# Solving the within-chunk system of an RWKV-7 scan by forward substitution over two 64-row halves, in place of completing the 128-row inverse

## What is computed

```python
def step(S, inp):
    r_t, w_t, k_t, v_t, kk_t, a_t = inp
    sa = jnp.einsum('bhij,bhj->bhi', S, -kk_t)
    S = (S * w_t[:, :, None, :]
         + sa[..., None] * (kk_t * a_t)[:, :, None, :]
         + v_t[..., None] * k_t[:, :, None, :])
    y = jnp.einsum('bhij,bhj->bhi', S, r_t)
    return S, y

S0 = jnp.zeros((b, RWKV_HEADS, RWKV_HEAD_DIM, RWKV_HEAD_DIM), F32)
_, ys = lax.scan(step, S0, (tmajor(rh), tmajor(wh), tmajor(kh), tmajor(vh), tmajor(kk), tmajor(ah)))
```

## Time and profile before

| | |
|---|---|
| median of 3 runs | 1505.27 us (1505.21 to 1505.7) |
| the profiled execution | 1507.26 us, its span 1505.4 us |
| TensorE busy | 98% of the span |
| VectorE, ScalarE busy | 83%, 67% |
| chunk 0's edited part | 429.9 to 445.2 us |
| chunk 1's edited part | 469.5 to 486.7 us |
| first expert product | 542.01 us |

### The profile page before, as it was taken

The page is one execution under the profiler, slowest core; times in us unless marked ns, Lnnn a source line. Parts: engine busy times, 40 slices in busy tenths (PEclk is TensorE's granted clock), DMA queues, the critical chain, the costliest instruction groups (busy, mean ns, idle before and its releaser), DMA issues.

```text
span 1505.4 us, 22041 instructions
## 1 busy us (share of the span) xinstructions
PE 1474.2 (98%) x8088; PEld 1226.9 (82%) x8088; DVE 1242.6 (83%) x1375; ACT 1009.8 (67%) x1157; POOL 22.2 (1%) x19
## 2 busy tenths in 40 slices
PE   8999999999899999999999999999999999999997
PEld 5888888799798588888888888888888888888885
DVE  3756666787885289999999999999999999999997
ACT  2544444663523178888888888888888878888885
POOL 0000000000000020000000000000000000000200
PEclk9999999999999999999999999999999999999998
DMA  9889553036405499999999999999999999999990
GB/s 361 326 271 301 175 168 112 1 117 217 141 2 178 174 322 372 395 392 395 396 392 396 394 368 388 390 365 383 394 366 373 393 386 362 395 380 362 349 369 28
DMA packets 206696, 453.57 MB, mean 301 GB/s; under 512 B 8881, under 2 KB 46257, under 8 KB 206386
## 3 DMA queue, kind: packets, MB, share of 16 engines
q1 hardware_dynamic: 203154, 446.12, 80.6%
q0 software_dynamic: 1280, 4.20, 1.1%
q10 hardware_dynamic: 2208, 2.50, 0.5%
HBM read 437.58 MB, written 23.60 MB: 306 GB/s over the span
## 4 chain that ended last, share of the span: by engine, by line
PE 92%; DVE 5%; ACT 2%; DMA 1%; issue 0%; DVEq 0%; ACTq 0%
PE psum L1591 20%; PE psum L1593 20%; PE psum L1592 20%; PE psum L2401 5%; PE psum L2404 3%; PE psum L902 2%; PE psum L2325 2%; PE psum L2365 2%; PE psum L2366 2%; PE psum L2367 2%; PE psum L600 2%; PE psum L1609 2%; PE psum L2318 1%; PE psum L696 1%; DVE time_mix_parts L1150 1%; PE psum L722 1%
## 5 line engine op out<-in xcount | busy, mean ns | idle before, releaser
L1799 DVE TENSOR_TENSOR w_lo<-ring,w_hi 128x1024 fp32r<-128x1024 f32 x672 | 811.0, 1224 | 63.5 <-ACT w_hi L1693 15.8
L1693 ACT ACTIVATE w_hi<-ring 128x1024 fp32r<-128x1024 f32 x672 | 711.3, 1062 | 172.5 <-PE psum L1593 172.4
L1591 PE MATMUL psum<-w_hi,xg_split 128*128 128x512 f32 x896 | 353.5, 395 | 0.3 <-DVE xg_split L1890 0.3
L1593 PE MATMUL psum<-w_lo,xg_split 128*128 128x512 f32 x896 | 349.4, 390 | 0.0
L1592 PE MATMUL psum<-w_hi,xg_split 128*128 128x512 f32 x896 | 348.8, 389 | 0.0
L1593 PEld LDWEIGHTS psum<-w_lo,xg_split 128*128 128x128 f32 x896 | 168.1, 188 | 35.8
L1591 PEld LDWEIGHTS psum<-w_hi,xg_split 128*128 128x128 f32 x896 | 168.3, 188 | 34.1 <-DVE xg_split L1890 0.6
L1592 PEld LDWEIGHTS psum<-w_hi,xg_split 128*128 128x128 f32 x896 | 168.4, 188 | 33.6
L1591 PE MATMUL psum<-w_hi,ht_split 128*128 128x512 f32 x448 | 176.0, 393 | 0.0
L1593 PE MATMUL psum<-w_lo,ht_split 128*128 128x512 f32 x448 | 174.6, 390 | 0.0
L1592 PE MATMUL psum<-w_hi,ht_split 128*128 128x512 f32 x448 | 174.4, 389 | 0.0
(11 more groups left out here) (370 smaller groups left out, 1488.7 us busy)
## 6 DMA issues: line engine op xcount, KB each, us to landing
ring<-o_moe_wg_dram SPq DMA_DIRECT2D x56, 2048.0 KB, 10.8
ring<-o_moe_wu_dram SPq DMA_DIRECT2D x56, 2048.0 KB, 11.3
ring<-o_moe_wd_dram SPq DMA_DIRECT2D x56, 2048.0 KB, 11.3
ring<-e_ffn_wg_dram SPq DMA_DIRECT2D x11, 1024.0 KB, 5.5
ring<-e_ffn_wu_dram SPq DMA_DIRECT2D x11, 1024.0 KB, 8.7
ring<-e_ffn_wd_dram SPq DMA_DIRECT2D x11, 1024.0 KB, 11.1
expert_rows<-work SPq DMA_DIRECT2D x1, 8192.0 KB, 27.9
ring<-e_w_in_dram SPq DMA_DIRECT2D x2, 2048.0 KB, 18.1
```

The costliest lines, as they stand in the source:

```text
L1591: nc.tensor.matmul(dst, x_hi, hi, start=first, stop=False)
L1593: return nc.tensor.matmul(dst, x_hi, lo, start=False, stop=last_)
L1693: nc.scalar.activation(w_hi[:, (4 * i + n) % 4, :], piece(i, n), ACT.Copy).then_inc(m_hi, 1)
L1799: V.tensor_tensor(w_lo[:, r, :], piece(i, n), w_hi[:, r, :].bitcast(F32), ALU.subtract).then_inc(m_lo, 1)
```

## The change

The top level of the inverse is taken out. What is left of XT are two inverses of 64 rows on its diagonal, and the system is solved by halves: the top half of U is the top inverse times the top half of R; the product of the matrix's lower left block with it is added to the low half of R on TensorE (third product of a head); then the low inverse gives the low half of U. `turned(c, 2)`, `top_Y` and `top_X` go, with their copies. `right_side` and `solved` run for a pair and a half. ScalarE, not VectorE, copies the solutions, 64 rows at a time, into `Us`, which now lies beside `Rs` in the ring. The masks of chunk 0 come one step earlier in VectorE's list. GpSimd's clearing of `Y6` goes, and with it one wait; so does the wait for the end of `recur(1, r)` ahead of chunk 0's solve.

```diff
-            def top_Y(c):
...
-            def top_X(c):
...
-            def solved(c):
-                for pair in range(2):
-                    pe.wait_ge(t_rc, 2 * c + pair + 1)
-                    pe.wait_ge(l_x6, 2 * c + pair + 1)
-                    for gg, l, k, o, at in heads_of(pair):
-                        last = nc.tensor.matmul(psum[:, (6, 0)[c] + pair, at:at + HD], XT[c][:, gg, l, :],
-                                                Rs[:, gg, HD * l:HD * l + HD], start=True, stop=True)
-                    last.then_inc(t_u, 1)
+            top, low = slice(0, HD), slice(HD, P)
+
+            def solved(c, pair, rows):
+                if rows == top:
+                    pe.wait_ge(l_xd, masked_at(c, 1, pair))
+                    pe.wait_ge(t_rc, 4 * c + pair + 1)
+                else:
+                    pe.wait_ge(t_rc, 4 * c + 2 + pair + 1)
+                for gg, l, k, o, at in heads_of(pair):
+                    last = nc.tensor.matmul(psum[rows, 4 + pair, at:at + HD], XT[c][rows, gg, l, rows],
+                                            Rs[rows, gg, HD * l:HD * l + HD], start=True, stop=True)
+                last.then_inc(t_u, 1)
+
+            def right_side(c, pair, rows):
+                pe.wait_ge(a_pm, 4 * c + 2 * pair + 2)
+                if rows == low:
+                    pe.wait_ge(t_uc, 4 * c + pair + 1)
+                upto = slice(0, rows.stop)
+                for gg, l, k, o, at in heads_of(pair):
+                    dst = psum[rows, pair, at:at + HD]
+                    vv = v_row[upto, c * D + k * P + o:c * D + k * P + o + HD]
+                    last = nc.tensor.matmul(dst, A_all[c][upto, gg, l, 2, rows], vv, start=True, stop=(c == 0 and rows == top))
+                    if c == 1:
+                        last = nc.tensor.matmul(dst, AR[:, k, c, 0, rows], ST[:, k, o:o + HD], start=False, stop=(rows == top))
+                    if rows == low:
+                        last = nc.tensor.matmul(dst, A_all[c][top, gg, l, 0, low], Us[top, gg, HD * l:HD * l + HD],
+                                                start=False, stop=True)
+                last.then_inc(t_r, 1)
...
+            right_side(0, 0, top)
             block_rows(1, 3)
-            turned(0, 2)
-            right_side(0, 0)
-            pe.wait_ge(y_zero, 3)
-            top_Y(0)
+            right_side(0, 1, top)
+            solved(0, 0, top)
+            solved(0, 1, top)
             block_rows(1, 4)
-            right_side(0, 1)
-            top_X(0)
-            pe.wait_ge(rec_done, 2)
-            solved(0)
+            for pair in range(2):
+                right_side(0, pair, low)
+            for pair in range(2):
+                solved(0, pair, low)
             outputs(0)
...
-            turned(1, 2)
-            right_side(1, 0)
-            top_Y(1)
-            right_side(1, 1)
-            top_X(1)
-            solved(1)
+            for rows in (top, low):
+                for pair in range(2):
+                    right_side(1, pair, rows)
+                for pair in range(2):
+                    solved(1, pair, rows)
             outputs(1)
...
+            def solved(c, pair, half):
+                rows = slice(HD * half, HD * half + HD)
+                act.wait_ge(t_u, 4 * c + 2 * half + pair + 1)
+                nc.scalar.activation(Us[rows, 2 * pair:2 * pair + 2, :], r3(psum[rows, 4 + pair, :], 2),
+                                     ACT.Copy).then_inc(t_uc, 1)
...
             recur(1, 3)
+            masked(0, 0)
             level_Y(0, 1, 0)
-            masked(0, 0)
+            masked(0, 1)
             level_Y(0, 1, 1)
-            masked(0, 1)
+            masked(0, 2)
             level_X(0, 1, 0)
-            masked(0, 2)
+            masked(0, 3)
             level_X(0, 1, 1)
-            masked(0, 3)
```

More of the change, by code:

```diff
@@ L416, in trunk @@
         s_part, s_col = sem("column_product"), sem("column_added")
-        l_tr, l_xe, l_y, l_yd, l_ya, l_xu, l_xd, l_x6 = (sem(x) for x in (
-            "level_T", "level_T_copied", "level_Y", "level_Y_masked", "top_Y_copied", "level_X", "level_X_added",
-            "top_X_copied"))
+        l_tr, l_xe, l_y, l_yd, l_xu, l_xd = (sem(x) for x in (
+            "level_T", "level_T_copied", "level_Y", "level_Y_masked", "level_X", "level_X_added"))
         y_zero, b_done, gw_done = sem("level_Y_zeroed"), sem("bonus_gated"), sem("gate_weighted")
@@ L473, in trunk @@
         Xv = [wu(3, 1024, 1024 * v).rearrange("p (g l t) -> p g l t", g=4, l=4) for v in range(2)]
-        Y6 = ru(13, 1024).rearrange("p (g n) -> p g n", g=4)
         Rs = ru(13, 1024, 1024).rearrange("p (g n) -> p g n", g=4)
@@ L477, in trunk @@
         pick = flatT[:, 0:(B0 - 1) * P]
-        Us = flatT[:, 0:1024].rearrange("p (g n) -> p g n", g=4)
+        Us = ru(13, 1024).rearrange("p (g n) -> p g n", g=4)
         gsq = flatT[:, 1024:2048].rearrange("p (k t) -> p k t", k=KT)
@@ L514, in lev @@
         def lev(c, v, pair):
-            return 6 * c + 2 * v + pair + 1
+            return 4 * c + 2 * v + pair + 1
         def masked_at(c, v, pair):
@@ L522, in turned_at @@
         def turned_at(c, v, n):
-            return 12 * c + 4 * v + n + 1
+            return 8 * c + 4 * v + n + 1
         TURN_BANK = (0, 1, 4, 5)
@@ L743, in rwkv_pe @@
             products(15)
-            def right_side(c, pair):
-                pe.wait_ge(a_pm, 4 * c + 2 * pair + 2)
-                pe.wait_ge(l_xe, turned_at(c, 2, pair))
-                for gg, l, k, o, at in heads_of(pair):
[L749 to L754, removed]
             pe.wait_ge(a_ma, 16)
@@ L758, in rwkv_pe @@
                 nc.tensor.transpose(psum[:, 2, 0:P], ident, ident)
-            pe.wait_ge(y_zero, 3)
+            pe.wait_ge(y_zero, 2)
             def turned(c, v):
@@ L766, in turned @@
                             pe.wait_ge(t_sc, 2)
-                    elif v == 2 and gg >= 2:
-                        pe.wait_ge(l_xd, masked_at(c, 1, 1))
                     else:
@@ L826, in outputs @@
             def outputs(c):
                 for pair in range(2):
-                    pe.wait_ge(t_uc, 2 * c + pair + 1)
+                    pe.wait_ge(t_uc, 4 * c + 2 + pair + 1)
                     pe.wait_ge(a_pm, 4 * c + 2 * pair + 2)
@@ L886, in rwkv_pe @@
             level_X(1, 1, 1)
-            turned(1, 2)
-            right_side(1, 0)
-            top_Y(1)
-            right_side(1, 1)
-            top_X(1)
-            solved(1)
+            for rows in (top, low):
[3 more added lines that the diff above has]
+                    solved(1, pair, rows)
             outputs(1)
             pe.wait_ge(t_yc, 4)
-            pe.wait_ge(l_x6, 4)
             gn_mean(1, 4)
@@ L1044, in copied, with right_side @@
                     nc.scalar.activation(a_home(s_), psum[:, bank:bank + 2, :], ACT.Copy).then_inc(a_ma, 1)
-            def right_side(c, pair):
-                act.wait_ge(t_r, 2 * c + pair + 1)
-                nc.scalar.activation(Rs[:, 2 * pair:2 * pair + 2, :], r3(psum[:, pair, :], 2),
+            def right_side(c, pair, half):
+                rows = slice(HD * half, HD * half + HD)
+                act.wait_ge(t_r, 4 * c + 2 * half + pair + 1)
+                nc.scalar.activation(Rs[rows, 2 * pair:2 * pair + 2, :], r3(psum[rows, pair, :], 2),
                                      ACT.Copy).then_inc(t_rc, 1)
+            def solved(c, pair, half):
+                rows = slice(HD * half, HD * half + HD)
+                act.wait_ge(t_u, 4 * c + 2 * half + pair + 1)
+                nc.scalar.activation(Us[rows, 2 * pair:2 * pair + 2, :], r3(psum[rows, 4 + pair, :], 2),
+                                     ACT.Copy).then_inc(t_uc, 1)
             def turned(c, v):
@@ L1056, in turned @@
                     nc.scalar.activation(dst, even, ACT.Copy).then_inc(l_xe, 1)
[L1058 to L1068, removed]
             def outputs(c):
@@ L1097, in rwkv_act @@
             turned(0, 1)
[L1098 to L1102, removed]
+            for half in range(2):
+                for pair in range(2):
+                    right_side(0, pair, half)
+                for pair in range(2):
+                    solved(0, pair, half)
             outputs(0)
@@ L1112, in rwkv_act @@
             last.then_inc(gw_done, 1)
[L1113 to L1117, removed]
+            for half in range(2):
+                for pair in range(2):
+                    right_side(1, pair, half)
+                for pair in range(2):
+                    solved(1, pair, half)
             outputs(1)
@@ L1320, in level_X @@
                 last.then_inc(l_xd, 1)
[L1322 to L1325, removed]
             def gn_centre(c, bank):
@@ L1413, in rwkv_pool @@
             nc.gpsimd.memset(zero_rows, 0.0).then_inc(x_zero, 1)
-            pool.wait_ge(a_mm, 16)
-            pool.wait_ge(bk_tr, 4)
-            nc.gpsimd.memset(Y6[0:HD, :, :], 0.0).then_inc(y_zero, 1)
```

(2 more changed lines are left out.)

## The result

| | before | changed |
|---|---|---|
| median | 1505.41 us (4 runs, 1505.21 to 1505.7) | 1530.01 us (4 runs, 1528.62 to 1532.65) |
| ratio | | 1.0165, 95% interval 1.0148 to 1.0183 |
| span of the profiled execution | 1505.4 us | 1528.1 us |
| first expert product | 542.01 us | 564.86 us |

What follows compares the result with a forecast made beforehand. TensorE's matrix work was taken as the bound. Chunk 1 +5.0, chunk 0 +0.6 and copies +0.1 give +5.7, record by record 5.5; +5.6 on the median 1505.27 gives 1510.9 us, range 1505.5 to 1515.

Steps and rivals of the forecast that it cites:

- the price of a change of shape: TensorE, 64-column records: each switch between 64-row and 128-row products costs 0.14 us.
- the count: Edited parts: chunk 1 has 224 records and 65 changes of shape, chunk 0 160 records, block rows and 32 changes.
- rival C: Alternating stretch lowers TensorE's clock: 5 to 10 us more if half of chunk 1's 22 us is slow, about 1518; chance 0.06.
- 0.6 forecast: Chunk 0's edited part: 16.0 us after the change against 15.3, beginning 0.1 earlier, so +0.6 us.
- 5.0 forecast: Chunk 1's edited part: 22.1 us after the change against 17.16, so +5.0 us.
- ScalarE's copies hide: Half copies of 0.59 us on ScalarE are covered by the other pair's solve; 0.1 us added in all.
- the masks' move: Chunk 0's fourth mask, one step earlier, is in time for pair 1's top right side; left in place it would cost 1.0 us.
- dropping VectorE's copies and GpSimd's memset: VectorE's four copies of U and GpSimd's memset with its wait go: 0 us.
- the delay reaches the end whole: What follows outputs is released by outputs, so the edited parts' delay passes undiminished to the kernel's end.
- Rivals A and B: A: 64-row beside 128-row products need no drain, 1497.7, chance 0.09. B: changes cost only half, 1506.1, chance 0.09.
- The check that I named: Changed timeline, right sides: pieces of two records with L805 and L807 follow 0.26 us from piece to piece.
- clock 1.00 there: Sign in the changed timeline: TensorE's granted clock stays 1.00 in the edited stretches of both chunks.

Runs made afterwards that it cites:

- filled kernel: The changed kernel with most right-side products done twice, the extra one into a bank that nothing reads: 1525.42 us, ratio 1.0134.
- two heads grouped: The changed kernel with each right side's products grouped by shape over two heads at a time, 49 changes of shape instead of 97: 1505.01 us, ratio 0.9993.
- grouped kernel: The changed kernel with a right side's products grouped by shape over a pair's eight heads, one start per bank: 1499.26 us, ratio 0.9969.
- top half in one shape: The changed kernel with chunk 1's top right-side product with A contracting over 128 rows, 31 changes of shape fewer: 1511.8 us, ratio 1.0047.
- masks back: The grouped kernel with chunk 0's four masks at their old places in VectorE's list: median 1503.63 us, ratio 0.999.
- fewest changes: The grouped kernel with chunk 1's top A over 128 rows and low-half products needing the top solution last for both pairs: 1499.77 us, ratio 0.9957.

## Why the prediction was wrong

- **Direction and the price of a change of shape: right.** The 0.14 us a change, put together from two other pairs of shapes, holds between 64x64 and 128x64 too, the pair that no row before showed: groups of two at 0.26 us at full clock instead of 0.12. Seen with the clock held, the count is right as well: 1525.4 us against 1524 in the filled kernel, 1505.0 against 1504 with two heads grouped, 14.3 and 12.2 us in the grouped one. The +5.6 us were right, but they are less than a quarter of the loss. The Trainium skill's rule in "TensorEngine Tiling (Array Packing)", Key Properties, that a change of mode drains the engine, agrees with these runs as far as they go: they show 0.14 us lost at each change, and not the drain itself.
- **The step that failed is rival C**: "Against: 1.00 throughout 430 to 486. Chance 0.06", and its price, "If half of chunk 1's 22 us ran at the lower clock". The 1.00 of those rows belonged to the stream that the change takes away. The new stream, two records in 0.26 us with a change of shape in each group, has no row before. (The solve before, at 0.112 a record, had 2.3 in that time, no change, and the full clock.) The row that was nearest in kind, the lower clock after the short products ahead of 531, spoke for a fall. I read that row and weighed it too low, though it wasn't a sure sign either: the grouped kernel has the same products and its trace no fall there. What the runs showed in place of the clock of 1.00 is one of 0.50 in both chunks, and that is the larger part of the loss, 4.4 and 11.4 us in the edited parts alone. The price that the prediction gave C, 5 to 10 us for chunk 1 alone, left chunk 0 out, and the range's upper edge, 1515, came from a dearer change of shape, with C left outside it.
- **The size**, from the two traces: chunk 0's part, from the last product of level v = 1 to the outputs, 449.38 - 427.09 = 22.3 us against 17.3 (in the trace before, its last product begins at 427.9 and the outputs at 445.16): +5.0, of it 0.6 forecast and 4.4 clock. From there to chunk 1 +1.0, the clock coming back only within the outputs. Chunk 1 +16.4, of it 5.0 forecast and 11.4 clock. Later parts up to the first expert product +1.2: the outputs of chunk 1 begin at the low clock, while the fall at 531 in the trace before doesn't come up in this one. Sum 23.6, less the 0.8 by which this execution was ahead at 427: 22.8, the difference of the expert products, 564.86 - 542.01. The medians are 24.6 apart because the trace before is of an execution of 1507.26 us, 1.9 above its median.
- **The rest held.** ScalarE's copies hide (0.59 us each, and TensorE is never idle from 430 to 440 and from 460 to 482 in the grouped kernel), the masks' move is worth 0.9 where 1.0 was said, dropping VectorE's copies and GpSimd's memset shows nowhere on the chain, and the delay reaches the end whole. Rivals A and B are refuted by the 0.26 us. The check that I named, groups of 0.26 us, would have read as right only for the first 3.1 us of alternation in chunk 0 and the first 4.4 in chunk 1; the other, "clock 1.00 there", is the one that failed.
- Open: what it is in a stream that decides. The runs give streams that kept the clock (groups of four records at 0.37 us; four and two by turns; the solve before, a record each 0.112) and streams that lost it (two and two at 0.26; 16 columns in each 0.11), and nothing between.

## What to carry to other kernels

Count the changes of the stationary operand's shape, not only the records: each cost 0.14 us here, and a loop with the shapes inside and the heads outside pays it per head. Then look at the clock of the new stream, not of the one replaced: with a change of shape at every second record, TensorE went to half speed and the loss became more than four times as large, although every view of busy time called it busy. The cure was the order of two loops, which turned the same products from 1.65% slower to 0.31% faster.

## What wasn't expected of the hardware

Two streams of equal busy share got different clocks: PE is 100% busy in both, but 1.00 was granted to groups of four records between changes and 0.50 to groups of two. Once down, the low solve's plain stream of 31 records at 0.11 us didn't bring it back in 3.5 us, nor did chunk 1's low half in 16 us, which kept the full clock when it started with it; in the changed kernel it came back only within the outputs, whose products stream 128 columns, 2.4 us after they began in chunk 0 and 4.9 in chunk 1. And more work took less time: 192 records added, 4.6 us gained.

The stream just ahead doesn't settle the clock alone. In three of the ten traces (top half in one shape, masks back, fewest changes) it fell for 3.2 to 3.4 us behind level v = 0 of chunk 1, and the sixteen transposes there took 3.5 to 3.6 us; in the other seven, with the same products ahead of them, they took 2.0. Such a fall costs 1.5 us, a quarter of what the grouping gains over the kernel before. So a gain of a microsecond has to be read from the part of the timeline that it concerns, not from the total.
